# Diagonal matmuls for seventeen convolution taps, and a shifted layer norm with sums taken tile by tile

## The chip, the core and the metric

The kernel runs on one core of a Trainium2 chip. The metric is the device time of one execution in microseconds (us). Three runs of the kernel before gave 1783.36, 1778.57 and 1788.19 us, so the median is 1783.36.

The core has a matmul engine (PE), a vector engine (DVE), an activation engine (ACT), GpSimd (POOL) and SyncE (SP), which issues most of the weight loads. Each runs its own stream in order. Semaphores join the streams.

## The reference, cut to what matters

The model has two blocks: an FFN, a mixer and an FFN, and then an "even" and an "odd" mixer. The change touches the odd mixer alone. It works on 512 positions and 1024 channels (8 channel tiles of 128):

```python
proj = h @ w_in                                   # 1024 -> 3 * 1024: val, gt, z
g = val * sigmoid(gt)
c = causal_depthwise_conv(g, conv_w) + conv_b     # 31 taps, each channel by itself
mu = mean(c, over channels)
cc = c - mu
var = mean(cc * cc, over channels)
c = cc * rsqrt(var + 1e-5) * ln_g + ln_b
y = silu(c) * silu(z)
x = x + y @ w_out
```

The result is normalised once more (RMS norm) and stored.

## The kernel before, in words

**Layout.** Activations are kept as channels on 128 partitions by 512 positions. Weights come from memory as 128x1024 fp32 tiles, in a ring of four (`w_stage`). ACT rounds each to `w_hi` (`hi`, L729), and DVE takes `w_lo = w_stage - w_hi` (`lo`, L1102). Each product is three matmuls: hi by hi, hi by lo, lo by hi (`three`, L1706 to L1708), 24 to a projected tile. Where fp32 operands are used directly, as with `ones` for a sum over channels, one matmul shows as two entries of the trace.

**The odd mixer** (`odd_mixer` in each engine's stream) has 24 projections, n = 0 to 23. For channel tile t, n = 3t gives the gate (ACT takes a Tanh of half of it, L1016), n = 3t+1 the value (DVE forms `gb`, L1623), and n = 3t+2 is z (ACT's Silu into `zo`, L1018). ACT's and DVE's loops run over the same n: pass n of each begins with the `hi` or `lo` of weight tile n+2. DVE's loop goes on to n = 26 without them.

**The convolution** of a tile is 31 taps. ACT does tap 0 with the bias into `pacc` (`first_tap`, L1059), and multiplies taps 1 to 13 (`tap`, L1052) into four buffers, from which POOL adds them to `pacc` (L713). DVE does taps 14 to 30 (`taps`, L1598 and L1601), alternately into the PSUM banks 4 and 5. A third of them stand in each of three passes, one tile behind. `merge` (L1608, L1609) adds `pacc` and both banks into `cv`. `gb` and `pacc` have two slots, so ACT can't begin the tap 0 of tile t before tile t-2 is merged. Tile 7's taps and merge follow the last projection.

**The layer norm.** PE multiplies `cv` by `ones` into bank 6, tile by tile (`mean`, L2101). When all eight tiles are in, DVE subtracts the mean (L1630), ACT squares (L1029), PE sums the squares in bank 7 (L2122), ACT takes Ln and Exp (L1031, L1033) for the inverse root, and DVE scales each tile (L1637). ACT applies Silu with the norm's gain and bias (L1042), DVE multiplies by `zo` (L1640), ACT rounds to `a_hi` (L1046) and DVE forms `a_lo` (L1644). Ln, Exp and Silu come from different function tables, so a table load precedes a change.

**The output projection** (`project_out_by_rows`) takes one `a` tile after another into all eight banks: rows 0 to 4 as they come, and the last three together. The ring lets weight tile j+4 be rounded when row j is done. In this stretch ACT and DVE prepare one weight tile and one row per pass.

Of the kernel before, what the change touches and what calls it, by code (L numbers as in the profile page):

```python
# [22 lines left out]
ALU = mybir.AluOpType  # L23
ACT = mybir.ActivationFunctionType

P = 128
S = 512
# [37 lines left out]
SEC = 3  # L65
GLU_TILES = [0, 2, 1, 3]
TAPS = 31
POOL_TAPS = 13


MH, AH, DH = 4, 8, 64
# [90 lines left out]
def build_program(nc, a, out):  # L162
    ctx = ExitStack()
    with ctx:  # L164
# [155 lines left out]

        put = region(arena, nc.sbuf_usable_end - arena)
        o_rows = put("o_rows", [P, ST, D])
        mats_d = nc.dram_tensor("mats_d", [4, P, SEC, MAT * P], F32).ap()

        put = region(at_of["a_hi"], HALF * S * 4)
# [58 lines left out]
        tap_prod = sem("tap_prod")  # L384
# [104 lines left out]
        def _(pool):  # L489
# [213 lines left out]
            def odd_mixer():  # L703
                pool.wait_ge(mix_ready, 2 * KT)
                pool.dma_start(cw_rows[:], a["conv_w_2"][0]).then_inc(cw_in, 16)
                pool.memset(ln_eps[:], 1e-5)
                pool.memset(gb[:, :, 0:TAPS - 1], 0.0).then_inc(odd_zero, 1)
                for t in range(KT):
                    pool.wait_ge(tap_ready, t + 1)
                    for m in range(t * POOL_TAPS, (t + 1) * POOL_TAPS):  # L710
# [10 lines left out]
        def _(act):  # L721
# [285 lines left out]
            def odd_mixer():  # L1007
                for n in range(3 * KT):
                    hi(0, T_ODD + n + 2)
                    act.wait_ge(w_used, T_ODD + n + 1)  # L1010
                    t = n // 3
                    if n == 0:
                        act.wait_ge(h_ready, 5 * KT)
                    if n % 3 == 0:
                        upto(act, g_ready, t - 1)
                        act.activation(tmp[:, t % 2], ps[n % 4][:], ACT.Tanh, scale=0.5).then_inc(odd_read, 1)  # L1016
                    if n % 3 == 2:
                        act.activation(zo[:, t], ps[n % 4][:], ACT.Silu).then_inc(odd_read, 1)  # L1018
                        first_tap(t)
                    for k in range(*[(4, 9), (9, POOL_TAPS), (0, 4)][n % 3]):  # L1020
                        if n >= 2:
                            tap(n // 3 - (n % 3 < 2), k)
                for k in range(4, POOL_TAPS):
                    tap(KT - 1, k)
                act.wait_ge(pool_tap, KT * POOL_TAPS)
                for t in range(KT):
                    act.wait_ge(cc_ready, t + 1)
                    upto(act, var_sum, t - 1)
                    act.activation(sq[:, t % 2], cv[:, t], ACT.Square).then_inc(cq_ready, 1)  # L1029
                act.wait_ge(var_sum, KT)  # L1030
                act.activation(rs[:], ps[7][:], ACT.Ln, bias=ln_eps[:], scale=1.0 / D).then_inc(lr_ready, 1)  # L1031
                act.wait_ge(lr_ready, 1)
                act.activation(rs[:], rs[:], ACT.Exp, scale=-0.5).then_inc(lr_ready, 1)  # L1033
                for t in range(KT + 1):
                    if t < 2:
                        hi(0, T_OOUT + 2 + t)
                    if t >= 3 and T_OOUT + t + 1 < T_END:
                        hi(0, T_OOUT + t + 1)
                    if t < KT:
                        act.wait_ge(cn_ready, t + 1)  # L1040
                        upto(act, yo_ready, t - 1)
                        act.activation(tmp[:, t % 2], cv[:, t], ACT.Silu, scale=cols[:, LN_G + t:LN_G + t + 1],  # L1042
                                       bias=cols[:, LN_B + t:LN_B + t + 1]).then_inc(cs_ready, 1)
                    if t >= 1:
                        act.wait_ge(yo_ready, t)
                        act.activation(a_hi[:, (t - 1) * S:t * S], zo[:, t - 1], ACT.Copy).then_inc(mix_hi, 1)  # L1046

            def tap(t, k):

                m = t * POOL_TAPS + k  # L1050
# [35 lines left out]
        def _(dve):  # L1086
# [492 lines left out]
            def odd_mixer():  # L1579
# [7 lines left out]
                first = 1 + POOL_TAPS  # L1587
                left = TAPS - first

                def taps(t, begin, end):  # L1590

                    dve.wait_ge(g_ready, t + 1)
                    for k in range(begin, end):
                        acc = ps[4 + (k - first) % 2][:]
                        upto(dve, tap_done, t * left + (k - first) - 1)
                        if k < first + 2:
                            upto(dve, cv_ready, t)
                            dve.tensor_scalar(acc, gb[:, t % 2, k:k + S], cw[:, t, k:k + 1], None, ALU.mult) \  # L1598
                                .then_inc(tap_done, 1)
                        else:  # L1600
                            dve.scalar_tensor_tensor(acc, gb[:, t % 2, k:k + S], cw[:, t, k:k + 1], acc,  # L1601
                                                     ALU.mult, ALU.add).then_inc(tap_done, 1)

                def merge(t):

                    dve.wait_ge(tap_done, (t + 1) * left)
                    dve.wait_ge(pool_tap, (t + 1) * POOL_TAPS)
                    link(dve.tensor_tensor(cv[:, t], pacc[:, t % 2], ps[4][:], ALU.add))  # L1608
                    dve.tensor_tensor(cv[:, t], cv[:, t], ps[5][:], ALU.add).then_inc(cv_ready, 1)  # L1609

                cut = [first, first + left // 3, first + 2 * left // 3, TAPS]
                for n in range(3 * KT + 3):
                    if n < 3 * KT:
                        lo(0, T_ODD + n + 2)
                    t = n // 3
                    if n % 3 == 0 and t >= 2:
                        merge(t - 2)
                    if n % 3 == 1 and n < 3 * KT:
                        dve.wait_ge(w_used, T_ODD + n + 1)
                        dve.wait_ge(odd_read, 2 * t + 1)  # L1620
                        upto(dve, tap_done, (t - 1) * left)
                        upto(dve, tap_prod, (t - 1) * POOL_TAPS)
                        dve.scalar_tensor_tensor(gb[:, t % 2, TAPS - 1:], tmp[:, t % 2], 1.0, ps[n % 4][:],  # L1623
                                                 ALU.add, ALU.mult).then_inc(g_ready, 1)
                    if t:
                        taps(t - 1, cut[n % 3], cut[n % 3 + 1])
                merge(KT - 1)
                dve.wait_ge(mean_sum, KT)
                for t in range(KT):
                    dve.scalar_tensor_tensor(cv[:, t], ps[6][:], -1.0 / D, cv[:, t], ALU.mult, ALU.add) \  # L1630
                        .then_inc(cc_ready, 1)
                dve.wait_ge(lr_ready, 2)
                for t in range(KT + 2):
                    if t < 2:
# [43 lines left out]
        def _(pe):  # L1678
# [417 lines left out]
                    mm.then_inc(w_used, 1)  # L2096

            def odd_mixer():
                def mean(t):
                    pe.wait_ge(cv_ready, t + 1)  # L2100
# [7 lines left out]
                for n in range(3 * KT):  # L2108
# [16 lines left out]

# [67 lines left out]
```

## Time and profile before

| what | value |
| --- | --- |
| median of three runs | 1783.36 us |
| the profiled execution | 1791.0 us |
| its span | 1789.1 us |
| mean granted TensorE clock over the span | 0.95 |
| PE, DVE, ACT, POOL busy, of the span | 1632.2, 865.9, 636.8, 365.6 us |
| odd projections, first start | 1511.7 us |
| output projection, first matmul | 1719.71 us |
| last instruction's end | 1789.1 us |

Times in the rows are from the start of the span. A shape is partitions by elements. A busy share is an average over stages that have different limits, so the table says little about the odd mixer, and the rows by stage say more. A granted clock of 1.00 is 2.4 GHz and 0.50 is 1.2 GHz.

### The profile page before, as it was taken

To read this page: it belongs to the slowest core of one execution; us is meant where nothing else is said; L and a number is where in the kernel's file an instruction comes from. 1 tells how busy PE (TensorE), PEld (TensorE's weight loads), DVE (VectorE), ACT (ScalarE), POOL (GpSimd) and SP (SyncE) were. 2 spreads that over 40 slices of the span, in tenths; PEclk is the share of its full clock that TensorE was granted. 3 is DMA by queue.
4 is the path that set the end of the run, shared out by engine and by line. 5 is a ranking of instruction groups with operands and counts; after the bars stand their busy time and mean duration, and the time that the engine had idled before them with its cause. 6 is when DMAs were issued, how large, how long until landed. Compare 5 with 4: busy or idle time off the path is not lost. (4 is left out here: it accounts for less than half of the span.)

```text
span 1789.1 us, 18560 instructions
## 1 busy us (share of the span) xinstructions
PE 1632.2 (91%) x6851; PEld 1203.2 (67%) x6851; DVE 865.9 (48%) x1190; ACT 636.8 (36%) x907; POOL 365.6 (20%) x469
## 2 busy tenths in 40 slices
PE   4899999998999998889999999999899999988377
PEld 2688888886775554235688888888477776766155
DVE  4777246333533335454433433432444344699844
ACT  3322112223335542443433212222442223666442
POOL 3011000000000000002000878510001100799700
PEclk9899999999999997789999999999899999999689
DMA  9677435322321111002233243463032122222101
GB/s 350 192 268 264 144 108 170 94 93 69 93 67 34 36 42 47 1 0 54 61 116 95 97 132 102 128 220 94 24 107 95 49 85 59 84 82 81 37 24 47
DMA packets 202194, 176.33 MB, mean 99 GB/s; under 512 B 6907, under 2 KB 181319, under 8 KB 201606
## 3 DMA queue, kind: packets, MB, share of 16 engines
q1 hardware_dynamic: 186902, 121.87, 22.9%
q0 software_dynamic: 14064, 51.34, 8.2%
q10 hardware_dynamic: 1152, 2.10, 0.3%
q8 instruction: 49, 0.80, 0.2%
q14 instruction: 27, 0.22, 0.0%
HBM read 166.90 MB, written 8.39 MB: 98 GB/s over the span
## 5 line engine op out<-in xcount | busy, mean ns | idle before, releaser
L1706 PE MATMUL ps<-h_hi,w_hi 128*128 128x512 f32 x1224 | 491.8, 402 | 39.4 <-DVE h_lo L1142 27.2
L1707 PE MATMUL ps<-h_lo,w_hi 128*128 128x512 f32 x1224 | 482.6, 394 | 0.0
L1708 PE MATMUL ps<-h_hi,w_lo 128*128 128x512 f32 x1224 | 482.1, 394 | 0.0
L1102 DVE TENSOR_TENSOR w_lo<-w_stage,w_hi 128x1024 fp32r<-128x1024 f32 x225 | 297.5, 1335 | 316.0 <-ACT w_hi L729 313.7
L1706 PEld LDWEIGHTS ps<-h_hi,w_hi 128*128 128x128 f32 x1224 | 233.4, 191 | 112.6 <-issue 64.1
L729 ACT ACTIVATE w_hi<-w_stage 128x1024 fp32r<-128x1024 f32 x225 | 231.0, 1048 | 200.3 <-PE ps L1708 188.3
L1708 PEld LDWEIGHTS ps<-h_hi,w_lo 128*128 128x128 f32 x1224 | 233.2, 191 | 50.2
L1707 PEld LDWEIGHTS ps<-h_lo,w_hi 128*128 128x128 f32 x1224 | 233.6, 191 | 46.6 <-issue 0.2
L1706 PE MATMUL ps<-a_hi,w_hi 128*128 128x512 f32 x544 | 225.4, 414 | 19.2 <-DVE a_lo L1644 12.8
L1707 PE MATMUL ps<-a_lo,w_hi 128*128 128x512 f32 x544 | 214.4, 394 | 0.0
L1708 PE MATMUL ps<-a_hi,w_lo 128*128 128x512 f32 x544 | 214.3, 394 | 0.0
L1706 PEld LDWEIGHTS ps<-a_hi,w_hi 128*128 128x128 f32 x544 | 103.7, 191 | 49.8 <-issue 23.0
L1159 DVE TENSOR_TENSOR tmp<-tmp,ps 128x512 f32<-128x512 f32 x44 | 30.3, 688 | 203.5 <-PE ps L1708 203.5
L1707 PEld LDWEIGHTS ps<-a_lo,w_hi 128*128 128x128 f32 x544 | 103.7, 191 | 26.9 <-issue 6.0
L1708 PEld LDWEIGHTS ps<-a_hi,w_lo 128*128 128x128 f32 x544 | 103.5, 190 | 22.2
L766 ACT ACTIVATE a_hi<-tmp 128x512 fp32r<-128x512 f32 (+1 forms) x44 | 27.9, 633 | 236.5 <-DVE tmp L1159 236.5
L713 POOL TENSOR_TENSOR pacc<-pacc,tmp 128x512 f32<-128x512 f32 x52 | 76.5, 1471 | 76.9 <-ACT tmp L1052 72.7
L497 POOL DMA_DIRECT2D ada_w<-in_w_ada x72 | 38.2, 531 | 239.5 <-DVE ada_acc L1112 141.0
L734 ACT ACTIVATE sq<-xT 128x512 f32<-128x512 f32 x56 | 35.3, 631 | 131.5 <-PE ps L1693 101.1
L1115 DVE SCALAR_TENSOR_TENSOR ada_acc<-ada_w,cs,ada_acc 128x1024 f32<-128x1024 f32 x63 | 80.8, 1283 | 2.6
L1601 DVE SCALAR_TENSOR_TENSOR ps<-gb,cw,ps 128x512 f32<-128x512 f32 x120 | 80.9, 745 | 0.0
L713 POOL TENSOR_TENSOR pacc<-pacc,sq 128x512 f32<-128x512 f32 x52 | 75.7, 1456 | 4.3
(365 smaller groups left out, 1612.1 us busy)
## 6 DMA issues: line engine op xcount, KB each, us to landing
w_stage<-in_w_gu SPq DMA_DIRECT2D x88, 512.0 KB, 4.4
ada_w<-in_w_ada POOLq DMA_DIRECT2D x72, 512.0 KB, 6.4
w_stage<-in_w_down SPq DMA_DIRECT2D x44, 512.0 KB, 3.7
w_stage<-in_w_in SPq DMA_DIRECT2D x24, 512.0 KB, 3.8
w_stage<-in_odd_w_in SPq DMA_DIRECT2D x24, 512.0 KB, 3.7
w_stage<-in_even_w_in SPq DMA_DIRECT2D x16, 512.0 KB, 3.9
w_stage<-in_w_out SPq DMA_DIRECT2D x8, 512.0 KB, 4.0
mats<-mats_d POOLq DMA_DIRECT2D x4, 1024.0 KB, 7.8
```

The source lines that it names most:

```text
L497: pool.dma_start(ada_w[:, kt], a["w_ada"][0][kt * P:(kt + 1) * P, bass.ds(j * D, D)]) \
L713: pool.tensor_tensor(pacc[:, t % 2], pacc[:, t % 2], tap_of[m % 4], ALU.add).then_inc(pool_tap, 1)
L729: act.activation(w_hi[:, c % RING], w_in[:, c % RING], ACT.Copy).then_inc(w_hi_ready, 1)
L734: act.activation(sq[:, kt % 2], xT[:, kt], ACT.Square).then_inc(sq_ready, 1)
L766: act.activation(a_hi[:, bass.ds(i * (2 * S) + f * S, S)], tmp2[:, f % 2], ACT.Copy) \
L1102: dve.tensor_tensor(w_lo[:, c % RING], w_in[:, c % RING], w_hi[:, c % RING].bitcast(F32), ALU.subtract).then_inc(w_split, 1)
L1115: dve.scalar_tensor_tensor(acc, ada_w[:, kt], cs[:, kt:kt + 1], acc, ALU.mult, ALU.add).then_inc(ada_done, 1)
L1159: dve.tensor_tensor(tmp2[:, f % 2], tmp[:, f % 2], ps[2 * (f % 2) + 1][:], ALU.mult) \
L1601: dve.scalar_tensor_tensor(acc, gb[:, t % 2, k:k + S], cw[:, t, k:k + 1], acc, ALU.mult, ALU.add).then_inc(tap_done, 1)
L1706: pe.matmul(bank, w_hi[:, slot, k], rhs_hi, start=start, stop=False, skip_group_check=True)
L1707: pe.matmul(bank, w_hi[:, slot, k], rhs_lo, start=False, stop=False, skip_group_check=True)
L1708: return pe.matmul(bank, w_lo[:, slot, k], rhs_hi, start=False, stop=stop, skip_group_check=True)
```

## The change

Three things are done in the odd mixer.

**Taps.** In tiles 6 and 7, 8 and 9 taps go to PE, as fp32 matmuls of a diagonal 128x128 matrix (`dgc`, the tap's weights on the diagonal) with the shifted `gb`, into banks 0 and 1. ACT builds the 17 matrices from the identity, two per pass from n = 6. POOL's share is 13 in tiles 0 to 5, then 11 and 8. DVE's is 17, then 11 and 13. PE's eight of tile 6 stand between projections 22 and 23, the nine of tile 7 behind the last projection. Merges 6 and 7 have a third add.

**Shift.** The mean over tile 0's 128 channels is taken first (`m0n` is its negative). Tiles 0 and 1 get it added on DVE (`centre`, at n = 9). In tiles 2 to 7, DVE's first tap adds it. The variance is then mean of squares less square of mean, of the shifted values.

**Order.** ACT squares tile u inside the loop and PE sums it there; only the sums of tiles 6 and 7 follow. The two weight tiles that were prepared in the first passes behind the norm are prepared ahead of tile 7's square on ACT, and behind merge 7 on DVE. The table for Ln and Exp is loaded ahead of that square. The mean is subtracted tile by tile (`deviate`), two tiles ahead of the inverse root and the others in DVE's passes of the last loop.

```diff
-POOL_TAPS = 13
+PE_TAPS = [0] * 6 + [8, 9]
+POOL_TAPS = [13] * 6 + [11, 8]
+DVE_TAPS = [TAPS - 1 - p - q for p, q in zip(POOL_TAPS, PE_TAPS)]
+PE_OF = [(t, 1 + POOL_TAPS[t] + j) for t in range(8) for j in range(PE_TAPS[t])]
+def of_tiles(taps, t):
+    return sum(taps[:max(t, 0)])
...
@@ ACT, odd_mixer, pass n @@
+                    if n == 9:
+                        act.wait_ge(mean_sum, 1)
+                        act.activation(m0n[:], ps[6][:], ACT.Copy, scale=-1.0 / P).then_inc(m0_ready, 1)
+                    for u in range(KT - 2):
+                        if n == (10 + u if u < 2 else 3 * u + 7):
+                            square_of(u)
+                    if n >= 2:
+                        u = n // 3 - (n % 3 < 2)
+                        for k in range(*[(4, 9), (9, POOL_TAPS[u]), (0, 4)][n % 3]):
+                            tap(u, k)
+                    if 6 <= n < 6 + len(PE_OF) // 2 + 1:
+                        act.wait_ge(cw_ready, 1)
+                        for m in range(2 * (n - 6), min(2 * (n - 6) + 2, len(PE_OF))):
+                            u, k = PE_OF[m]
+                            act.activation(dgc[:, m], ident[:], ACT.Copy, scale=cw[:, u, k:k + 1]).then_inc(dgc_ready, 1)
@@ ACT, behind the loop @@
-                act.wait_ge(pool_tap, KT * POOL_TAPS)
-                for t in range(KT):
-                    act.wait_ge(cc_ready, t + 1)
-                    upto(act, var_sum, t - 1)
-                    act.activation(sq[:, t % 2], cv[:, t], ACT.Square).then_inc(cq_ready, 1)
-                act.wait_ge(var_sum, KT)
-                act.activation(rs[:], ps[7][:], ACT.Ln, bias=ln_eps[:], scale=1.0 / D).then_inc(lr_ready, 1)
-                act.wait_ge(lr_ready, 1)
+                square_of(KT - 2)
+                for n in range(2):
+                    hi(0, T_OOUT + 2 + n)
+                act.preload_act_table_set("natural_log_exp_and_others")
+                square_of(KT - 1)
+                act.wait_ge(mean_sum, 1 + KT)
+                act.wait_ge(var_sum, KT - 1)
+                act.activation(lsq[:, 0], ps[6][:], ACT.Square, scale=1.0 / D).then_inc(lr_ready, 1)
+                act.activation(m0n[:], ps[6][:], ACT.Copy, scale=-1.0 / D).then_inc(m0_ready, 1)
+                act.wait_ge(lr_ready, 2)
+                act.activation(rs[:], lsq[:, 0], ACT.Ln, bias=ln_eps[:]).then_inc(lr_ready, 1)
+                act.wait_ge(lr_ready, 3)
                 act.activation(rs[:], rs[:], ACT.Exp, scale=-0.5).then_inc(lr_ready, 1)
...
+            def square_of(t):
+                act.wait_ge(cc_ready if t < 2 else cv_ready, t + 1)
+                upto(act, var_sum, t - 1)
+                act.activation(lsq[:, t % 2], cv[:, t], ACT.Square).then_inc(cq_ready, 1)
@@ DVE, odd_mixer @@
+                        if k == first and t >= 2:
+                            dve.wait_ge(m0_ready, 1)
+                            dve.scalar_tensor_tensor(acc, gb[:, t % 2, k:k + S], cw[:, t, k:k + 1], m0n[:],
+                                                     ALU.mult, ALU.add).then_inc(tap_done, 1)
...
+                    if PE_TAPS[t]:
+                        dve.wait_ge(pool_tap, of_tiles(POOL_TAPS, t + 1))
+                        dve.wait_ge(pe_tap, t - 5)
+                        link(dve.tensor_tensor(cv[:, t], pacc[:, t % 2], ps[t - 6][:], ALU.add))
+                        link(dve.tensor_tensor(cv[:, t], cv[:, t], ps[4][:], ALU.add))
+                        dve.tensor_tensor(cv[:, t], cv[:, t], ps[5][:], ALU.add).then_inc(cv_ready, 1)
...
+                def centre(t):
+                    dve.wait_ge(cv_ready, t + 1)
+                    dve.wait_ge(m0_ready, 1)
+                    dve.tensor_tensor(cv[:, t], cv[:, t], m0n[:], ALU.add).then_inc(cc_ready, 1)
...
+                    if n == 9:
+                        centre(0)
+                        centre(1)
...
                 merge(KT - 1)
-                dve.wait_ge(mean_sum, KT)
-                for t in range(KT):
-                    dve.scalar_tensor_tensor(cv[:, t], ps[6][:], -1.0 / D, cv[:, t], ALU.mult, ALU.add) \
-                        .then_inc(cc_ready, 1)
-                dve.wait_ge(lr_ready, 2)
+                for n in range(2):
+                    lo(0, T_OOUT + 2 + n)
+                def deviate(t):
+                    dve.wait_ge(cv_ready, KT)
+                    dve.wait_ge(m0_ready, 2)
+                    return dve.tensor_tensor(cv[:, t], cv[:, t], m0n[:], ALU.add)
+                dve.wait_ge(lr_ready, 1)
+                dve.wait_ge(var_sum, KT)
+                dve.scalar_tensor_tensor(lsq[:, 0], ps[7][:], 1.0 / D, lsq[:, 0], ALU.mult, ALU.subtract).then_inc(lr_ready, 1)
+                for t in range(2):
+                    link(deviate(t))
+                dve.wait_ge(lr_ready, 4)
                 for t in range(KT + 2):
-                    if t < 2:
-                        lo(0, T_OOUT + 2 + t)
                     if t < KT:
+                        if t >= 2:
+                            link(deviate(t))
                         dve.tensor_tensor(cv[:, t], cv[:, t], rs[:], ALU.mult).then_inc(cn_ready, 1)
@@ PE, odd_mixer @@
+                def spread(t):
+                    pe.wait_ge(cq_ready, t + 1)
+                    pe.matmul(ps[7][:], ones[:], lsq[:, t % 2], start=(t == 0), stop=(t == KT - 1)).then_inc(var_sum, 1)
+                def pe_taps(t):
+                    first = of_tiles(PE_TAPS, t)
+                    pe.wait_ge(g_ready, t + 1)
+                    pe.wait_ge(dgc_ready, first + PE_TAPS[t])
+                    pe.wait_ge(odd_read, 2 * KT - 2 + t - 6)
+                    for j in range(PE_TAPS[t]):
+                        k = PE_OF[first + j][1]
+                        mm = pe.matmul(ps[t - 6][:], dgc[:, first + j], gb[:, t % 2, k:k + S],
+                                       start=(j == 0), stop=(j == PE_TAPS[t] - 1))
+                    mm.then_inc(pe_tap, 1)
...
-                    if n % 3 == 2 and n > 6:
+                    if n == 8:
+                        pe.wait_ge(cv_ready, 1)
+                        pe.matmul(ps[6][:], ones[:], cv[:, 0], start=True, stop=True).then_inc(mean_sum, 1)
+                    if n == 11:
+                        mean(0)
+                    if n % 3 == 2 and n >= 11:
                         mean(n // 3 - 2)
+                    if n == 12:
+                        spread(0)
+                    if n % 3 == 0 and n >= 12:
+                        spread(n // 3 - 3)
+                    if n == 3 * KT - 2:
+                        pe_taps(KT - 2)
+                spread(KT - 3)
+                pe_taps(KT - 1)
                 mean(KT - 2)
+                spread(KT - 2)
                 mean(KT - 1)
-                for t in range(KT):
-                    pe.wait_ge(cq_ready, t + 1)
-                    pe.matmul(ps[7][:], ones[:], sq[:, t % 2], start=(t == 0), stop=(t == KT - 1)).then_inc(var_sum, 1)
+                spread(KT - 1)
```

## Rows read from the trace of the kernel before

**Rows 1.** Windows: length, busy (x instructions) of PE/PEld/DVE/ACT/POOL, clock, DMA.

```profile
1634.30:1654.80 20.50, 17.99 (x76) 13.71 (x75) 19.22 (x25) 13.51 (x20) 19.39 (x13) 1.00 0.26 78
1654.80:1675.20 20.40, 9.85 (x41) 7.17 (x39) 19.14 (x25) 13.54 (x20) 19.25 (x13) 0.85 0.26 83
1675.20:1692.70 17.50, 2.08 (x2) 0.50 (x2) 14.01 (x22) 7.13 (x10) 16.47 (x13) 0.50 0.01 3
1692.70:1707.90 15.20, 12.18 (x18) 3.96 (x18) 6.25 (x10) 6.14 (x9) 0.00 (x0) 0.66 0.00 0
1707.90:1719.70 11.80, 0.00 (x0) 0.02 (x1) 6.19 (x9) 9.18 (x12) 0.00 (x0) 0.73 0.26 89
1719.70:1724.00 4.30, 4.29 (x11) 3.45 (x12) 1.67 (x3) 0.06 (x1) 0.00 (x0) 0.56 0.02 4
```

**Rows 2.** Chain that ended last, behind the last tap: start, us, what.

```profile
1692.72 0.70 DVE cv L1608
...
1694.18 2.09 PE ps L2101 x2
...
1697.76 8.21 PE ps L2122 x12
...
1706.71 1.28 ACT L1031
...
1710.00 0.63 ACT rs L1033
...
1711.68 1.23 DVE w_lo L1102
...
1719.71 0.77 PE ps L1706
```

**Rows 3.** Timeline of POOL: start, us; two pairs of adds.

```profile
1670.25 3.47 POOL L713 TENSOR_TENSOR pacc<-pacc,tmp 128x512 f32<-128x512 f32 x2
...
1676.55 2.62 POOL L713 TENSOR_TENSOR pacc<-pacc,tmp 128x512 f32<-128x512 f32 x2
```

**Rows 4.** Two lines of DVE: ns min/median/max, starts (L1163: 985 to 1200).

```profile
L1102 DVE TENSOR_TENSOR w_lo<-w_stage,w_hi x225: 1209/1226/2151, 41.4 to 1744.7; 128x1024 fp32r<-128x1024 f32 x113
...
L1163 DVE TENSOR_TENSOR a_lo<-tmp,a_hi x14: 692/694/1541, 986.1 to 1199.3; 128x512 fp32r<-128x512 f32 x14
```

**Rows 5.** Timeline of DVE and ACT, tiles 2 to 4.

```profile
1589.11 0.80 ACT L1059 ACTIVATE pacc<-gb,cols,cw 128x512 f32<-128x512 f32 x1
...
1597.18 0.68 DVE L1608 TENSOR_TENSOR cv<-pacc,ps 128x512 f32<-128x512 f32 x1
...
1601.81 1.04 ACT L729 ACTIVATE w_hi<-w_stage 128x1024 fp32r<-128x1024 f32 x1
```

**Rows 6.** Timeline: projections 22 and 23, zo 7, merge 6, tile 7's taps.

```profile
1652.37 0.47 PE L1706 MATMUL ps<-h_hi,w_hi 128*128 128x512 f32 x1 [0.66 <-DVE w_lo L1102]
...
1658.78 0.47 PE L1706 MATMUL ps<-h_hi,w_hi 128*128 128x512 f32 x1 [0.72 <-DVE w_lo L1102]
...
1670.43 0.57 ACT L1018 ACTIVATE zo<-ps 128x512 f32<-128x512 f32 x1
...
1676.59 0.69 DVE L1608 TENSOR_TENSOR cv<-pacc,ps 128x512 f32<-128x512 f32 x1
...
1679.45 9.96 DVE L1601 SCALAR_TENSOR_TENSOR ps<-gb,cw,ps 128x512 f32<-128x512 f32 x15
```

**Rows 7.** Groups of ACT (busy, mean ns); an fp32 matmul in the chain.

```profile
L849 ACT ACTIVATE e_m<-dg 128x128 f32<-128x128 f32 x32 | 9.5, 307 | 3.3 <-DVE p_m L1323 3.3
...
L1042 ACT ACTIVATE tmp<-cv,cols 128x512 f32<-128x512 f32 x8 | 6.5, 806 | 3.2 <-DVE cv L1637 3.2
...
1756.24 0.86 PE ps L1693 x2
```

**Rows 8.** Timeline: last weight split, and the wait before the last rows.

```profile
1744.71 1.22 DVE L1102 TENSOR_TENSOR w_lo<-w_stage,w_hi 128x1024 fp32r<-128x1024 f32 x1 [2.41 <-ACT w_hi L729]
...
1749.88 0.47 PE L1706 MATMUL ps<-a_hi,w_hi 128*128 128x512 f32 x1 [0.92 <-DVE a_lo L1644]
```

More of the change, by code:

```diff
@@ L322, in build_program @@
         o_rows = put("o_rows", [P, ST, D])
+        put = region(at_of["a_lo"] + 2 * S * 4, 6 * S * 4)
+        dgc = put("dgc", [P, sum(PE_TAPS), P])
+        put = region(at_of["a_hi"] + KT * S * 4, 3 * S * 4)
+        lsq = put("lsq", [P, 2, S])
+        m0n = put("m0n", [P, S])
         mats_d = nc.dram_tensor("mats_d", [4, P, SEC, MAT * P], F32).ap()
@@ L709, in odd_mixer @@
                     pool.wait_ge(tap_ready, t + 1)
-                    for m in range(t * POOL_TAPS, (t + 1) * POOL_TAPS):
+                    for m in range(of_tiles(POOL_TAPS, t), of_tiles(POOL_TAPS, t + 1)):
                         upto(pool, pool_tap, m)
@@ new lines, in odd_mixer @@
+                for k in range(4, POOL_TAPS[KT - 1]):
+                    tap(KT - 1, k)
+                square_of(KT - 2)
[6 more added lines that the diff above has]
+                act.activation(lsq[:, 0], ps[6][:], ACT.Square, scale=1.0 / D).then_inc(lr_ready, 1)
@@ L1586, in odd_mixer, with taps @@
                 dve.wait_ge(odd_zero, 1)
-                first = 1 + POOL_TAPS
-                left = TAPS - first
-                def taps(t, begin, end):
+                def taps(t, third):
+                    first = TAPS - DVE_TAPS[t]
+                    base = of_tiles(DVE_TAPS, t)
                     dve.wait_ge(g_ready, t + 1)
-                    for k in range(begin, end):
+                    for k in range(first + third * DVE_TAPS[t] // 3, first + (third + 1) * DVE_TAPS[t] // 3):
                         acc = ps[4 + (k - first) % 2][:]
-                        upto(dve, tap_done, t * left + (k - first) - 1)
+                        upto(dve, tap_done, base + (k - first) - 1)
                         if k < first + 2:
                             upto(dve, cv_ready, t)
+                        if k == first and t >= 2:
+                            dve.wait_ge(m0_ready, 1)
+                            dve.scalar_tensor_tensor(acc, gb[:, t % 2, k:k + S], cw[:, t, k:k + 1], m0n[:],
+                                                     ALU.mult, ALU.add).then_inc(tap_done, 1)
+                        elif k < first + 2:
                             dve.tensor_scalar(acc, gb[:, t % 2, k:k + S], cw[:, t, k:k + 1], None, ALU.mult) \
@@ L1604, in merge @@
                 def merge(t):
[L1606 to L1611, printed above, removed]
+                    dve.wait_ge(tap_done, of_tiles(DVE_TAPS, t + 1))
+                    if PE_TAPS[t]:
[4 more added lines that the diff above has]
+                        dve.tensor_tensor(cv[:, t], cv[:, t], ps[5][:], ALU.add).then_inc(cv_ready, 1)
+                    else:
+                        dve.wait_ge(pool_tap, of_tiles(POOL_TAPS, t + 1))
+                        link(dve.tensor_tensor(cv[:, t], pacc[:, t % 2], ps[4][:], ALU.add))
+                        dve.tensor_tensor(cv[:, t], cv[:, t], ps[5][:], ALU.add).then_inc(cv_ready, 1)
+                def centre(t):
+                    dve.wait_ge(cv_ready, t + 1)
+                    dve.wait_ge(m0_ready, 1)
+                    dve.tensor_tensor(cv[:, t], cv[:, t], m0n[:], ALU.add).then_inc(cc_ready, 1)
                 for n in range(3 * KT + 3):
@@ L1625, in odd_mixer @@
                     if t:
[L1626 removed]
+                        taps(t - 1, n % 3)
                 merge(KT - 1)
[L1628 to L1632 removed]
+                for n in range(2):
[10 more added lines that the diff above has]
+                dve.wait_ge(lr_ready, 4)
                 for t in range(KT + 2):
[L1634 to L1635 removed]
                     if t < KT:
+                        if t >= 2:
+                            link(deviate(t))
                         dve.tensor_tensor(cv[:, t], cv[:, t], rs[:], ALU.mult).then_inc(cn_ready, 1)
@@ L2098, in odd_mixer @@
             def odd_mixer():
+                def spread(t):
[11 more added lines that the diff above has]
+                    mm.then_inc(pe_tap, 1)
                 def mean(t):
-                    pe.wait_ge(cv_ready, t + 1)
+                    if t == 0:
+                        pe.wait_ge(m0_ready, 1)
+                    pe.wait_ge(cc_ready if t < 2 else cv_ready, t + 1)
                     pe.matmul(ps[6][:], ones[:], cv[:, t], start=(t == 0), stop=(t == KT - 1)).then_inc(mean_sum, 1)
```

13 lines of the change are left out of this document (4 added, 9 removed).

## The prediction

> **What bounds the kernel now.** I read the windows by stage first, then the chain that ended last, then single instructions on each engine. While the odd block projects, PE works in 18.0 of 20.5 us per tile, DVE in 19.2, POOL in 19.4; from 1654.8 PE empties, and for the 17.5 us from 1675.2 it works 2.1 us, while POOL is full [rows 1]. Up to its last tap the chain is POOL's 104 adds, back to back: a pair takes 2.62 us, and 3.47 when one of DVE's two-input subtractions meets it [rows 3]. Behind the last tap everything is serial: merge at 1692.72, a mean matmul of 2.09 (TensorE is at half rate, its granted clock in this stretch is 0.50, that is 1.2 GHz), eight squares and eight sums (8.21 of the chain), Ln and Exp with a table load each, a weight split, and the normalisation, until the output projection starts at 1719.71 [rows 1, 2]. So PE has nearly nothing to do between about 1664.5 and 1719.7. The change must be costed on POOL and DVE up to the last merge, and as serial latency after it. An improvement of PE's busy share would be worth nothing.
>
> **The sum is made against the profiled execution**, 1791.0 us (span 1789.1, 1.9 outside), which is 7.6 above the median of 1783.36. About 0.5% is what a measurement of this kernel can tell from no change.
>
> **1. Taps taken from POOL and DVE.** POOL loses 2 adds in tile 6 and 5 in tile 7. Each costs 1.345, as thirteen fill the 17.5 us of tile 7 [rows 1]: 2.7 and 6.7 us. DVE loses 6 taps in tile 6 and 4 in tile 7 at 0.66 (9.96 / 15 [rows 6]): 4.0 and 2.7 us.
>
> **2. New port trouble.** Two centring adds and the first tap of tiles 2 to 7 now read two SBUF tensors. The rows show what such an operation meets beside POOL: the 1024-wide subtraction goes from 1.23 to at most 2.15, the 512-wide one from 0.69 to 1.54 [rows 4], and POOL's pair grows by 0.85 [rows 3]. For a 512-wide one POOL's price lies between 0 and 0.85; I take 0.48 (0.85 x 0.69 / 1.23), as the two sizes differ only in length. DVE: 0.85 extra for each, the contended row. Seven such operations before tile 6 ends: POOL 3.4, DVE 2 x 1.54 + 5 x 0.85 = 7.3, of which DVE's own idle time (at most 1.3 per tile [rows 1], taken as 1 over five tiles) swallows 5. Tile 7 has one more: 0.48 and 0.85. The Trainium skill (SBUF — State Buffer, section "SBUF: two separate sides") says that the pair of ports is an exclusive lock, taken also by a DVE operation with two SBUF inputs, and that the loser waits for the whole of the other instruction. By that rule POOL would lose 0.69 eight times, 5.5 us in place of 3.9, a result 1 to 2 us later. The row, where a 1.23 us holder costs POOL 0.85, is kept.
>
> **3. Tile 6's end.** POOL: 1675.2 - 2.7 + 3.4 = 1675.9. DVE: 1676.6 [rows 6] - 4.0 + 2.3 = 1674.9. Merge 6 starts at 1675.9 and has three adds at 0.70 [rows 2], so 1678.0.
>
> **4. Work put on PE.** One fp32 matmul of 512 columns costs 0.86 at full rate [rows 7]. The mean of tile 0 and five sums of squares lie in the loop, 5.2 us together, against PE's 2.5 idle us per tile [rows 1]: nothing, except that PE runs some 2 us late with DVE. The eight diagonal matmuls of tile 6 stand between projections 22 and 23. Projection 22 ran from 1652.37, a projection is 5.7 (1658.78 less 1652.37 less 0.72), so it ended at 1658.1 [rows 6]; 2.1 later, plus 8 x 0.86 = 6.9, plus projection 23 at 5.7, gives 1672.8. ACT then needs Silu 0.57 [rows 6], the first tap 0.80 [rows 5] and one product, about 0.7: POOL can begin tile 7 at 1674.9, 1 us before it is free. That is the thinnest cover in the change; without it each us late is a us lost. The nine of tile 7 run after 1.7 us of sums and end at 1682.2, hidden by DVE's taps.
>
> **5. Work put on ACT.** Seventeen 128x128 copies at 0.31 [rows 7], six squares and one mean copy at about 0.63: 9.7 us in the loop, less 7 products. ACT is busy 13.5 of 20.5 per tile [rows 1]; covered by its waits for POOL. A square stands ahead of taps, and is reached after the merge it needs: merge 2 begins at 1597.18, ACT's thirteenth pass at 1601.81 [rows 5]. ACT's last product, square 6, two weight copies (now ahead of the last merge) and the table load end near 1686, covered by tile 7.
>
> **6. Last merge.** POOL: 1675.9 + 8 x 1.345 + 0.48 = 1687.1. DVE: 1678.0 + 13 x 0.66 + 0.85 = 1687.5. Merge 7 starts at 1687.5, 5.2 earlier than 1692.72, and its third add brings it to 1689.6, 4.5 before the old end at 1694.1.
>
> **7. From the last merge to the projection.** Old: 1694.1 to 1719.7, 25.6. New, in series: last mean 2.09; last sum 1.7 (twice 0.86, since PE has idled some 4.5 us and the half-rate row is the nearest); variance on DVE 0.7; Ln 0.7; Exp 0.65; one table load 1.28; Silu 0.8 [rows 7]; product 0.7; deviation and scaling of the next tile 1.3, its product 0.6; a_lo 0.65. Sum 11.2 (a 512-wide DVE operation is 0.60 pipelined, 0.70 alone [rows 2]). The two weight subtractions, 2 x 1.23, run beside mean and sum (3.8); if PE were at full rate they would show by 0.6. Gone are seven squares and sums, eight centrings on the path, Ln's and Exp's table loads (one hidden, one merged) and two copy-and-subtract pairs. Bounds: 9.6 with both matmuls at full rate, 13 with another half-rate us and DVE order losses. The projection starts at 1689.6 + 11.2 = 1700.8, 18.9 us early.
> The rows show each table load as 1.28 us, with Exp following at once [rows 2]. The Trainium skill (ScalarE: Activation LUTs, section "What ACT_TABLE_LOAD costs") adds a drain of about 1.38 us to every switch, 2.66 in all. By the page, two loads fewer would be worth 5.3 us in place of 2.6; the row decides.
>
> **8. Output projection.** DVE now subtracts the mean there, 0.72 per tile. It is hidden while PE works on earlier rows, but the last tiles' path already ends 0.92 late [rows 8]: 0.7 lost. The restart at half rate (4.3 us at mean clock 0.56 [rows 1]) stays, as PE has again been idle.
>
> **Sum:** 18.9 - 0.7 = 18.2, so 1772.8 for the profiled execution; against the median, 1783.36 - 18.2 = **1765 us**.
>
> **Rivals.**
> A. *More than that, 1760.* POOL and DVE meet less than priced (up to 2.5 us), the last matmuls run at full rate (1.6) and so does the restart (2). For: in the 11.8 us before the old projection, with PE idle, the mean granted clock was still 0.73 [rows 1]. Against: PE works too little just before. Chance 0.12.
> B. *PE becomes the bound, 1774.* The diagonal matmuls ahead of projection 23 delay ACT's Silu and first tap of tile 7. At the slow rate (2.09 each) the eight cost 16.7, 9.8 more; POOL starts 8.8 later, and the gain falls to 9.4. Decides: Silu of tile 7 later than 1674. Against: PE comes from a dense stretch at clock 1.00. Chance 0.08.
> C. *No change, 1783.* The last merge gains nothing, as DVE runs 5 us late, and the tail keeps a wait for the last sum at half rate. Nothing in the rows carries all of it. Chance 0.05.
> D. *Slower, 1793.* The squares close a ring: ACT waits for DVE's merge before it makes POOL's products, and PE waits for ACT's square before the next projection. POOL has four products in stock, 5.4 us; if every one of the six squares starves it for another 4.7, 28 us are lost and 18 gained. It decides when a merge ends over 5.4 us after ACT reaches its square. Against: today the merge starts 4.6 us earlier than ACT's pass, and DVE gets only some 3 later [rows 5]. Chance 0.03.
> The forecast keeps 0.72; its own spread comes from step 2 (-3, +3), step 7 (-1.6, +1.8) and the runs' own 5 us. Range 1757 to 1774. Faster by over 0.5% (below 1774.4): forecast, A and most of B, 0.90; same 0.07; slower 0.03.
>
> **What would show it.** Right: POOL adds end near 1687 and the L1706 on a_hi starts near 1701; Silu of tile 7 (zo) lies near 1673 with POOL's tile 7 unstarved; centring and two-input taps take about 1.5 us on DVE; no table load between Ln and Exp; the last mean and sum at half rate; the gap before the last three rows near 1.6. Wrong: POOL idle between taps, ACT waiting for cv inside the loop, the zo copy later than 1675, or an output projection that starts after 1705.

## The result, and the profile after

The changed kernel takes 1768.32 us in the median of four runs (1761.29 to 1773.01), beside 1784.36 for the kernel before (four runs). The ratio is 0.9907 with a 95% interval of 0.9885 to 0.9930, so it is faster by 16.6 us (12.5 to 20.5), 0.9%. The profiled execution takes 1773.0 us, 18.0 below the one of before.

Profiles differ by up to 8.5 us in code that the change doesn't touch, so positions are counted here from POOL's first add of tile 0 (1531.94 us before, 1531.36 after), and the end from the output projection's first matmul:

| counted from POOL's first add, us | before | after |
| --- | --- | --- |
| `zo` of tile 7 begins | 138.5 | 140.7 |
| POOL's last add ends | 160.7 | 154.1 |
| last merge begins | 160.8 | 155.6 |
| last merge ends | 162.2 | 157.7 |
| output projection's first matmul | 187.8 | 169.0 |
| from there to the end of the span | 69.4 | 71.0 |

So 4.5 us were gained up to the last merge and 14.3 behind it (25.6 became 11.3), and 1.6 were given back in the output projection and behind it. These three, with 0.6 us that the unchanged part happened to take less, make the 17.8 by which the spans differ. Counted from POOL's first add to the end of the span, the change itself is worth 17.2.

The chain that ended last, after the change, from the last merge to the projection (start, us, what):

```profile
1665.07 1.05 ACT w_hi L746
...
1686.91 0.70 DVE cv L1652
1687.63 0.70 DVE cv L1653
1688.36 0.70 DVE cv L1654
1689.10 2.07 PE ps L2185 x2
1691.17 1.44 PE ps L2168 x2
1692.71 0.70 DVE lsq L1696
1693.44 0.73 ACT rs L1064
1694.19 0.63 ACT rs L1066
1694.84 1.28 ACT L1073
1696.13 0.82 ACT tmp L1073
...
1697.59 0.70 DVE cv L1692
...
1698.92 0.69 DVE zo L1707
1699.61 0.61 DVE a_lo L1711
1700.35 0.77 PE ps L1773
```

Against [rows 2], POOL's chain is gone from the last 22 us before the merge: at 1665.07 it is an ACT copy of a weight tile, and from 1666.14 DVE alone. Behind the merge there is one mean, one sum, one variance, Ln and Exp in one piece, one table load, and the first row.

The same stretch by windows, which answers to [rows 1] (length, busy and instructions of PE, PEld, DVE, ACT, POOL, then clock and DMA):

```profile
1659.50:1685.00 25.50, 23.70 (x67) 12.26 (x66) 23.41 (x31) 16.51 (x23) 24.19 (x17) 1.00 0.21 63
1685.00:1689.10 4.10, 0.00 (x1) 0.00 (x1) 4.00 (x7) 0.02 (x1) 0.51 (x1) 0.54 0.00 0
1689.10:1692.70 3.60, 3.50 (x4) 1.17 (x4) 2.21 (x2) 1.69 (x3) 0.00 (x0) 0.57 0.33 101
1692.70:1700.30 7.60, 0.00 (x0) 0.00 (x0) 6.56 (x11) 6.05 (x8) 0.00 (x0) 0.69 0.27 90
1700.30:1706.00 5.70, 5.65 (x14) 4.48 (x15) 2.40 (x4) 0.07 (x1) 0.00 (x0) 0.51 0.00 0
```

PE is full to 1683 now, at a granted clock of 1.00. It idles from there to 1689.1, the mean and sum run at 0.57, and the projection starts at 0.51.

The instructions that the shift added, on DVE and ACT (ns min/median/max), which answer to [rows 4] and [rows 7]:

```profile
L1637 DVE SCALAR_TENSOR_TENSOR ps<-gb,cw,m0n x6: 800/1555/1786, 1580.9 to 1678.2; 128x512 f32<-128x512 f32 x6
```

```profile
L1664 DVE TENSOR_TENSOR cv<-cv,m0n x2: 1776/1805/1834, 1577.5 to 1579.2; 128x512 f32<-128x512 f32 x2
```

```profile
L1051 ACT ACTIVATE dgc<-ident,cw x17: 384/387/389, 1560.3 to 1615.4; 128x128 f32<-128x128 f32 x17
```

The first taps with the mean take 1.56 us in the median and the two centring adds 1.78 and 1.83, where an undisturbed operation of that length takes 0.69. The diagonal matrices took 0.39 each. On POOL's side a pair of adds with one such tap in it takes 2.95 us in place of some 2.65, and one with a 1024-wide weight subtraction 3.52:

```profile
1662.81 2.95 POOL L730 TENSOR_TENSOR pacc<-pacc,sq 128x512 f32<-128x512 f32 x2
1665.84 3.52 POOL L730 TENSOR_TENSOR pacc<-pacc,tmp 128x512 f32<-128x512 f32 x2
```

Exactly eight of POOL's 97 adds take 1.60 to 1.62 us where an undisturbed one takes 1.27 to 1.30, and each of them overlaps one of the eight operations that the shift added. So such an operation costs POOL about 0.33 us. A weight subtraction costs it 0.86 (2.15 less 1.29). In both sizes that is the operation's own undisturbed time (0.69 and 1.23) less 0.36 or 0.37; two sizes are few for a rule, but the price isn't proportional to the length.

The timeline around tile 6's end, which answers to [rows 6]:

```profile
1659.54 7.03 PE L2177 MATMUL ps<-gb,dgc 128*128 128x512 f32 x16
...
1666.14 2.06 DVE L1139 TENSOR_TENSOR w_lo<-w_stage,w_hi 128x1024 fp32r<-128x1024 f32 x1 [1.54 <-ACT w_hi L746]
...
1672.07 0.60 ACT L1035 ACTIVATE zo<-ps 128x512 f32<-128x512 f32 x1 [3.25 <-PE ps L1775]
...
1675.85 0.69 DVE L1652 TENSOR_TENSOR cv<-pacc,ps 128x512 f32<-128x512 f32 x1
```

Merge 6 starts when DVE's taps are done; POOL's last add of tile 6 ended at 1674.31, 1.5 us earlier. DVE idles 1.54 us for a weight tile, and ACT 3.25 for projection 23, behind the eight diagonal matmuls. In the output projection, the wait before the last three rows has grown from 0.92 [rows 8] to 1.63:

```profile
1732.08 0.47 PE L1773 MATMUL ps<-a_hi,w_hi 128*128 128x512 f32 x1 [1.63 <-DVE a_lo L1711]
```

### The profile page after: what moved, and what is told of

Its sections match the earlier page's. It is cut to its first block and busy times, and to the rows that moved or that the text cites. A ratio compares the mean times of both kernels' runs of the same rounds, so it can differ in the third digit from the quotient of the medians.

```text
span 1771.3 us, 18641 instructions
## 1 busy us (share of the span) xinstructions
PE 1643.6 (93%) x6887; PEld 1210.1 (68%) x6887; DVE 865.6 (49%) x1185; ACT 635.4 (36%) x919; POOL 359.4 (20%) x462
## 5 line engine op out<-in xcount | busy, mean ns | idle before, releaser
L1139 DVE TENSOR_TENSOR w_lo<-w_stage,w_hi 128x1024 fp32r<-128x1024 f32 x225 | 292.9, 1315 | 301.2 <-ACT w_hi L746 299.0
L730 POOL TENSOR_TENSOR pacc<-pacc,tmp 128x512 f32<-128x512 f32 x49 | 72.4, 1477 | 76.7 <-ACT tmp L1089 72.7
L1643 DVE SCALAR_TENSOR_TENSOR ps<-gb,cw,ps 128x512 f32<-128x512 f32 x110 | 74.3, 744 | 0.0
```

The costliest lines, as they stand in the source:

```text
L1139: dve.tensor_tensor(w_lo[:, c % RING], w_in[:, c % RING], w_hi[:, c % RING].bitcast(F32), ALU.subtract).then_inc(w_split, 1)
```

## The experiments

Positions are from POOL's first add, as above. The expectations of the first three runs count from the odd mixer's first projection, which lies 20.3 us ahead of POOL's first add in the kernel before, the change and the taps alone, and 21.2 and 21.3 us in the norm alone and the run without the shift, since their PE was at half rate for longer there; differences are read from POOL's add. Times are medians, and "before" was run along with each group (1783.3, 1782.4 and 1783.2 us). The early table load, the late projection and the two more taps on PE were executed once each (1770.06, 1767.52 and 1768.48 us); one time of a kernel that moves by over 5 us tells nothing, and their positions alone are read.

### The taps alone

```diff
 # the change, with the norm of before; in words, not the kernel's lines
-    square_of(u), spread(u), centre(0), centre(1), deviate(t), the early table load
-    first tap of tiles 2 to 7: + m0n
+    mean over all tiles; centre, square and sum behind the last merge
```

> The tap split of the change with the layer norm of before: no shift, all squares and sums behind the last merge, no early table load. All positions are counted from the first projection of the odd mixer (before: last merge ends at 182.5, output projection starts at 208.0; the change: 178.0 and 189.3). Theory: the taps alone are worth more than they show in the change, because no two-input operation of DVE meets POOL. Projection 22 ends at 146.4 as before, the eight diagonal matmuls and projection 23 bring the zo copy of tile 7 to 158.9, POOL starts tile 7 at 160.9 and DVE's thirteen taps end at 171.8, so the last merge ends at 174.0. The tail stays 25.6, the output projection starts at 199.6, the time is 8.4 us below before. Rival: the ports cost nothing, and the merge ends at 178 as in the change; then the time is 4.5 us below before.

Measured: 1775.59 us, ratio 0.9952 (0.9933 to 0.9970). `zo` of tile 7 begins at 138.5, POOL's last add ends at 151.3, the last merge ends at 155.0 and the projection starts at 180.8: 7.0 us early, with a tail of 25.8. The rival (the ports cost nothing, and the merge ends where the change has it) is out, since the merge ends 2.7 us earlier than in the change. But it came 1.3 later than the theory's. DVE's timeline says where that went, here and in the kernel before:

```profile
1655.89 0.74 DVE L1631 SCALAR_TENSOR_TENSOR ps<-gb,cw,ps 128x512 f32<-128x512 f32 x1
1658.68 2.04 DVE L1131 TENSOR_TENSOR w_lo<-w_stage,w_hi 128x1024 fp32r<-128x1024 f32 x1 [2.04 <-ACT w_hi L746]
...
1668.37 0.69 DVE L1640 TENSOR_TENSOR cv<-pacc,ps 128x512 f32<-128x512 f32 x1
...
1671.95 7.33 DVE L1631 SCALAR_TENSOR_TENSOR ps<-gb,cw,ps 128x512 f32<-128x512 f32 x11
1679.32 0.69 DVE L1640 TENSOR_TENSOR cv<-pacc,ps 128x512 f32<-128x512 f32 x1
```

```profile
1664.27 2.07 DVE L1102 TENSOR_TENSOR w_lo<-w_stage,w_hi 128x1024 fp32r<-128x1024 f32 x1 [0.79 <-ACT w_hi L729]
```

In the pass that holds three of tile 6's taps in place of five, DVE waits 2.04 us for the next weight tile, where it waited 0.79 before. ACT begins to round that tile at 131.2 in both kernels, counted from POOL's first add, behind products that wait for POOL's adds; DVE gets there 1.3 us earlier and gains nothing by it. So 1.25 of the 4.0 us that were taken from DVE in tile 6 turn into this wait (merge 6 comes 2.7 earlier and not 4.0), and merge 7 then begins 1.6 us after POOL is done: DVE, not POOL, bounds the last merge. What an earlier rounding of that tile would gain was not run.

### The norm alone

```diff
-PE_TAPS = [0] * 6 + [8, 9]
-POOL_TAPS = [13] * 6 + [11, 8]
+PE_TAPS = [0] * 8
+POOL_TAPS = [13] * 8
```

> The shifted norm, its early sums and its new order, with the taps of before (13 on POOL, 17 on DVE, none on PE). Theory: the shift's eight two-input operations lengthen POOL's chain by 2.9 us (what the change's POOL shows beyond seven fewer adds), so the last merge ends at 185.4; the tail takes 11.3, the output projection starts at 196.7 against 208.0, and 1.6 us are given back behind it: 9.7 us below before. Rival: the shift costs nothing on POOL, the merge ends at 182.5 and the time is 12.6 below before. If the two halves of the change simply add, e1 and e2 together make about 18.

Measured: 1776.19 us, ratio 0.9958 (0.9940 to 0.9976). The last merge ends at 165.3, 3.1 later than before (theory 2.9), the tail is 11.3, the projection starts at 176.7, 11.1 early, and what follows takes 71.0, 1.6 more than before. That is 9.5 net where the theory had 9.7; the rival's 12.6 is out. From POOL's first add to the end the taps alone make 6.9 and the norm alone 9.5, and the whole makes 17.2, so they add within 1 us. The tail's gain of 14.2 us stands here without the taps.

### Without the shift

```diff
 # in words, not the kernel's lines
-    if n == 9: m0n = -mean of tile 0; centre(0); centre(1)
-    first tap of tiles 2 to 7: scalar_tensor_tensor(..., m0n[:], ALU.mult, ALU.add)
+    first tap of all tiles: tensor_scalar(..., ALU.mult)
```

> The change without the shift: the first tile's mean, the two centring adds and the added mean in the first taps of tiles 2 to 7 are left out; the variance is mean of squares less square of mean of the values as they are, the same quantity. Theory: the contended operations delay DVE and POOL by 4 us net; without them the zo copy of tile 7 comes at about 159 in place of 161.0, the last merge ends at 174.0 in place of 178.0, and the time is 4.0 us below the change, 20 below before. Rival 1: DVE's idle time hides them, at most 1 us. Rival 2: the wait for the eight diagonal matmuls takes their place, since ACT needs projection 23: then the zo copy stays at 161 and the gain is 1 to 2 us.

Measured: 1766.47 us, ratio to before 0.9892 (0.9862 to 0.9922). The medians can't tell this from the change (0.9885 to 0.9930), the positions can. `zo` of tile 7 comes at 138.6 in place of 140.7, as the theory had it, and POOL ends at 151.4 in place of 154.1, but the merge gains 2.5 and not 4.0: DVE waits 2.05 us for the same weight tile as with the taps alone. Neither rival fits. So the shift costs POOL 2.7 us for eight operations, 0.34 each, and the last merge 2.5. (With the norm alone it is 3.1 on POOL.)

### The early table load

```diff
-                act.preload_act_table_set("natural_log_exp_and_others")
```

> The change without the early table load: Ln and Exp each load their own table behind the last sums, as in the kernel before. Theory: a load is 1.28 us and nothing more. Ln's load starts when ACT has copied the mean (3.2 us behind the last merge in the change) and ends about 0.2 late for Ln; Exp's 1.28 lies bare; so the output projection starts 1.4 to 1.6 us later than in the change. Rival (a drain of 1.38 beside each load): 2.9 for Ln's and 2.7 for Exp's of which 1.4 is covered, so 4.2 us later.

Measured: the tail is 12.75 where the change has 11.31, 1.44 more, as the theory had it. ACT's timeline:

```profile
1687.44 0.59 ACT L1061 ACTIVATE m0n<-ps 128x512 f32<-128x512 f32 x1
1688.05 1.28 ACT L1063 ACT_TABLE_LOAD   x1
1689.34 0.72 ACT L1063 ACTIVATE rs<-lsq,ln_eps 128x512 f32<-128x512 f32 x1
1690.08 1.28 ACT L1065 ACT_TABLE_LOAD   x1
1691.38 0.63 ACT L1065 ACTIVATE rs<-rs 128x512 f32<-128x512 f32 x1
1692.02 1.28 ACT L1072 ACT_TABLE_LOAD   x1
```

Each load begins when the activation before it ends, and the next activation begins 0.02 us behind the load. No drain shows beside it. The Trainium skill (ScalarE: Activation LUTs, "What ACT_TABLE_LOAD costs") adds a drain of about 1.38 us to every switch; by that rule the estimate was 4.2 us more, and the measured 1.44 says that it doesn't hold for these loads.

### Idle matmuls that keep PE busy

```diff
                 spread(KT - 2)
+                busy(7)    # fp32 matmuls of ones and gb into bank 2, read by nobody
                 mean(KT - 1)
                 spread(KT - 1)
+                busy(8)
```

> The change with fp32 matmuls of no use put on PE, into a free bank: seven between the sum of tile 6 and the last mean, eight behind the last sum. Theory: PE's granted clock stays at 1.00 up to the output projection. The last mean and sum take 1.9 in place of 3.6 us, of which 1.4 counts (DVE's two weight subtractions then end last), and the 5.5 us of half-rate restart cost 2.7 less: 4.1 us less time than the change. Rival 1: such matmuls don't hold the clock, and the time stays. Rival 2: the seven end later than the last merge and delay the mean, 0 to 0.5 us given back.

Measured: 1761.70 us, ratio to before 0.9861 (0.9812 to 0.9911). The tail is 9.8 in place of 11.3, and what follows 68.3 in place of 71.0: 4.1 us together, as the theory said. Counted from POOL's first add it is 3.8, since this execution already had `zo` of tile 7 0.3 us later, ahead of the first idle matmul. The ratios of the two kernels to before overlap, so the gain over the change is read from the positions. PE's timeline and the windows:

```profile
1675.38 6.17 PE L2217 MATMUL ps<-gb,ones 128*128 128x512 f32 x14
1681.46 1.13 PE L2185 MATMUL ps<-cv,ones 128*128 128x512 f32 x2
1682.43 1.02 PE L2168 MATMUL ps<-lsq,ones 128*128 128x512 f32 x2
1683.29 7.03 PE L2217 MATMUL ps<-gb,ones 128*128 128x512 f32 x16
1691.23 0.47 PE L1773 MATMUL ps<-a_hi,w_hi 128*128 128x512 f32 x1 [0.92 <-DVE a_lo L1711]
```

```profile
1675.00:1681.40 6.40, 6.40 (x16) 2.60 (x14) 6.30 (x11) 1.92 (x2) 2.73 (x3) 1.00 0.00 0
1681.40:1683.30 1.90, 1.90 (x6) 0.88 (x6) 1.90 (x3) 1.30 (x3) 0.00 (x0) 1.00 0.00 0
1683.30:1691.20 7.90, 7.02 (x17) 2.82 (x15) 6.87 (x12) 6.48 (x9) 0.00 (x0) 1.00 0.38 133
1691.20:1697.00 5.80, 5.77 (x25) 4.80 (x26) 2.38 (x4) 0.05 (x1) 0.00 (x0) 1.00 0.00 0
```

The granted clock is 1.00 in all four. The mean takes 1.13 in place of 2.07 us, and the projection starts at full rate, where the change needs 5.5 us to get there.

### Projection 23 later

```diff
+                    if t == KT - 2:
+                        for j in range(4):
+                            pe.matmul(ps[0][:], ones[:], gb[:, 0, 0:S], start=True, stop=True)
                     for j in range(PE_TAPS[t]):
```

> The change with four more fp32 matmuls of no use ahead of the eight diagonal ones of tile 6, so that projection 23 comes 3.4 us later. Theory: POOL has 0.4 us of cover at its first add of tile 7 and ends 1.4 ahead of DVE, so of the 3.4 some 1.7 reach the last merge and the output projection. Rival 1: the cover is as wide as the delay, nothing moves. Rival 2: PE bounds the stage and all 3.4 arrive.

Measured: `zo` of tile 7 begins 3.7 later, POOL's last add ends 3.4 later, the merge ends 2.1 later and the projection starts 2.3 later. The cover of POOL's first add is 0.3 us, near the 0.4 that the theory gave it, and all the rest of the delay reaches POOL:

```profile
1659.49 3.60 PE L2180 MATMUL ps<-gb,dgc 128*128 128x512 f32 x8
...
1668.59 0.60 ACT L1035 ACTIVATE zo<-ps 128x512 f32<-128x512 f32 x1 [6.68 <-PE ps L1775]
...
1670.66 1.27 POOL L730 TENSOR_TENSOR pacc<-pacc,tmp 128x512 f32<-128x512 f32 x1 [3.26 <-ACT tmp L1089]
...
1680.46 1.26 POOL L730 TENSOR_TENSOR pacc<-pacc,tmp 128x512 f32<-128x512 f32 x1
1681.81 0.69 DVE L1652 TENSOR_TENSOR cv<-pacc,ps 128x512 f32<-128x512 f32 x1 [1.42 <-issue]
```

POOL idles 3.26 us, and the merge now follows its last add at once. The other part of the theory holds: 1.3 of POOL's delay is swallowed, because DVE was the later one. The theory's 1.7 at the end became 2.3: the delay was 3.7 and not 3.4, the cover 0.1 thinner, and the tail 0.3 longer, which no experiment explains. Neither rival fits: something moves, and not all of it. PE doesn't bound the stage in the change.

### Two more of tile 7's taps on PE

```diff
-PE_TAPS = [0] * 6 + [8, 9]
+PE_TAPS = [0] * 6 + [8, 11]
```

> The change with eleven of tile 7's taps on PE in place of nine, and eleven on DVE in place of thirteen. Theory: DVE bounds the last merge, by 1.4 us over POOL; two taps at 0.66 fewer bring merge and output projection 1.3 us earlier, while PE's eleven end at 1683, before the merge. Rival: POOL or ACT bounds the merge, and it stays.

Measured: the last merge begins at 154.5 in place of 155.6, where POOL's last add ends at 154.4, and the projection starts 1.5 earlier. The merge has 1.05 of this: two taps are worth 1.3, and POOL, free at 154.4, stops it there. The other 0.4 is in the tail, and comes with the clock. PE had idled 2.9 us and not 5.9 when the last mean came, and the mean took 1.37 us in place of 2.07:

```profile
1685.38 1.37 PE L2185 MATMUL ps<-cv,ones 128*128 128x512 f32 x2 [2.92 <-DVE cv L1654]
```

The rival (POOL or ACT bounds, and the merge stays) is out, and from here on POOL is the bound.

### The three together

The edits of the runs without the shift, with idle matmuls (three and eight) and with eleven taps on PE.

> The change without the shift, with eleven of tile 7's taps on PE and eleven on DVE, and with idle matmuls that keep PE busy (three ahead of the last mean, eight behind the last sum). Counted from POOL's first add (before: last merge ends at 162.2, output projection starts at 187.8, 69.4 follow; the change: 157.7, 169.0, 71.0). If the three effects add: DVE starts merge 7 at 151.7, just behind POOL (151.4), it ends at 153.9, the tail is 9.8, the projection starts at 163.7 and 68.4 follow: 7.8 us below the change, 25 below before. Rival 1: POOL or the wait for projection 23 takes the bound, and the merge stays at 155.2 as in the run without the shift. Rival 2: PE's eleven diagonal matmuls, the mean and sum of tile 6 and the three idle ones end after the merge, and the tail grows by 1.

Measured: 1759.51 us, ratio to before 0.9858 (0.9838 to 0.9879). The last merge ends at 153.8, the tail is 9.8, the projection starts at 163.6, 68.5 follow. All four were forecast within 0.2, and both rivals are out. Counted that way it is 7.9 us below the change and 25.1 below the kernel before. It is faster than both, and its ratio lies clear of the change's (0.9885 to 0.9930); from the run with idle matmuls the ratios can't tell it.

### The subtraction of the mean one pass earlier

```diff
@@ the run before this one, output projection @@
-                        if t >= 2:
-                            link(deviate(t))
...
+                    if 1 <= t < KT - 1:
+                        link(deviate(t + 1))
                     if t >= 3 and T_OOUT + t + 1 < T_END:
                         lo(0, T_OOUT + t + 1)
```

> The run before this one with DVE's subtraction of the mean done one pass earlier in the output projection, ahead of the wait for the next weight tile, where DVE idles 2.4 us. Theory: the subtraction of tile 7 lies on the path that ends with the last a_lo, so the wait before the last three rows falls from 1.63 to 0.92 and the time by 0.7 us; the first a_lo comes another 0.6 earlier, since the subtraction of tile 2 no longer stands ahead of it. 1.3 together. Rival: the subtraction then delays a weight tile, and nothing is gained.

Measured: 1759.10 us, ratio to before 0.9858 (0.9836 to 0.9880), not to be told from the run before it. PE's wait before the last three rows is 0.99 in place of 1.63, and from the projection to the end 68.0 in place of 68.5. The second half of the theory fell: the first matmul stayed (163.7 after 163.6), because tile 2's subtraction still stands ahead of the first `a_lo`, now behind the first product. The wait in the run before this one, and here:

```profile
1720.80 0.47 PE L1763 MATMUL ps<-a_hi,w_hi 128*128 128x512 f32 x1 [1.63 <-DVE a_lo L1701]
```

```profile
1718.43 0.47 PE L1763 MATMUL ps<-a_hi,w_hi 128*128 128x512 f32 x1 [0.99 <-DVE a_lo L1699]
```

## Why the prediction was right

The forecast was 1765 (1757 to 1774); 1768.3 was measured. It gave 18.2 us against the profiled execution, which moved by 18.0; 0.8 of that is unchanged code and time outside the span, so 17.2 answer to the 18.2. The medians moved by 16.0, and the interval of the ratio (12.5 to 20.5) holds all of these. The mechanism was right: the gain came where it was placed, on POOL and DVE up to the last merge and as latency behind it. The start of the last merge came out to the tenth by errors that cancelled (steps 3 and 6). By its steps (times of the prediction less 0.6, since the unchanged part was shorter):

- **1, taps.** The sizes held. What the step left out is that DVE's time saved in tile 6 doesn't all arrive: its wait for a weight tile grew from 0.79 us to 2.04 with the taps alone and to 1.54 in the change. Without the shift merge 6 came 2.6 us earlier, and not 4.0.
- **2, ports.** The direction was right and the sizes mixed. The centring adds took 1.8 us, not 1.54, and the first taps 0.80 to 1.79. POOL lost 0.34 an operation (2.7 in all) where 0.48 (3.9) were priced; the step scaled the 0.85 with the length, and the runs show the undisturbed time less 0.36. The merge paid 2.5. The rule of the Trainium skill (SBUF — State Buffer, "SBUF: two separate sides") is right on who collides: merges, which have one PSUM operand, kept their 0.69 beside POOL. Its "exclusive lock" for the whole instruction would, by the prediction's estimate, have cost POOL 5.5 us, twice what the runs show.
- **3, tile 6.** Merge 6 was to start at 1675.3 and did at 1675.85, but this was luck. The step named POOL as the later engine, at 1675.3, and DVE at 1674.3. POOL was done at 1674.31, 1.0 early by step 2; DVE was ready at 1675.85, 1.5 late, by the weight tile of step 1.
- **4, PE.** `zo` of tile 7 was to start at 1672.2 and did at 1672.07. The cover was said to be 1 us. It was 0.3: the first product of tile 7 was ready at 1673.98 and POOL free at 1674.31, and in the delayed run 3.7 us at `zo` made POOL's last add 3.4 later. POOL came earlier than summed, so the cover was thinner.
- **5, ACT.** The matrices took 0.39, not 0.31, and were covered: POOL never idled over 0.13 us between its 97 adds. No square held up a product: of ACT's eight, one alone waited, the last (4.50 us, for merge 7).
- **6, last merge.** Forecast start 1686.9, measured 1686.91. That DVE is the later one was right, POOL's sum being 1 us too late by step 2. The exact hit is two errors of DVE's sum: it began 0.55 late, at merge 6, and its thirteen taps took 0.5 less, since the first of them paid 0.1 and not 0.85 for the port.
- **7, tail.** Forecast 11.2, measured 11.3. The last mean and sum ran at half rate as assumed (2.07 and 1.44 of the chain, 2.09 and 1.7 in the sum), and undoing it gave the bound of 9.8 (forecast 9.6).
- **8, output projection.** The longer wait was 0.71 (forecast 0.7). "The restart at half rate stays" was 0.8 short, the one term that was put at nothing: the stretch with a matmul every 0.43 us, where it is 0.23 behind it, took 5.5 us (1700.35 to 1705.81) in place of 3.8 (1719.71 to 1723.47), and about half of the 1.7 more is lost. That length isn't the change's own: with the same output projection it was 3.3 us in the runs with the late projection and with eleven taps, and 70.3 and 70.5 us followed in place of 71.0. What sets it stays open.

**Rivals.** A (more) lived on the clock at full rate and on cheaper ports. The clock was at half rate, and the run with idle matmuls shows what that part was worth, 4.1 us (priced at 3.6); the ports did cost POOL 1.2 less than priced, but DVE bounded the last merge, so nothing came of it. B (PE bounds) is the one that came nearest to deciding: with four matmuls more, POOL starved. The slow-rate price never came, as the clock was 1.00 there. C and D didn't come: the last merge gained 4.5 us, and ACT never waited for a merge inside the loop.

## What to carry to other kernels

Work taken from the last tiles of a pipeline counts only on the engine that is later at each join, so write down both engines' times at every merge, and with them the waits for what a third engine delivers at its own pace; here POOL's 104 adds filled the chain before, and DVE bounded it after. In a serial tail, count latencies one by one: squares and sums that can be taken tile by tile and table loads that can be merged or stand ahead of a wait gave 14.3 of the 18.8 us (of which the early load has 1.4; the rest was not taken apart). Where the matmul engine must wait some microseconds ahead of dense work, look at the granted clock of the first matmuls, and price idle matmuls against it.

## What the runs showed of the hardware

- Fp32 matmuls with no use, put where PE waits, kept the granted clock at 1.00. From the last merge to the end this kernel took 4.1 us less, without any other change.
- A DVE operation of 512 columns with two SBUF inputs took 0.80 to 1.83 us beside POOL's adds and 0.69 without them, and cost one of POOL's adds 0.33 us; one of 1024 columns (1.23 undisturbed) cost it 0.86. With one input in PSUM (the merges, 0.69) neither paid.
- A function-table load cost 1.28 us and nothing beside it, three times in a row.
- The same code ahead of the odd mixer took between 1503 and 1512 us up to the first projection in these profiles, so a median of a few runs moves by more than several of the effects here; positions inside the stage repeat within 0.3 us. Behind the projection's start they don't: 70.3 to 71.2 us followed in six executions of the same output projection.
